# Column norms at the transitions of a fused two-block kernel, sums of squares in a PSUM bank, and a first merge in another order

## The reference, cut to what matters

```python
# first block
mix = merge(o_na, o_g, og, m_a, m_b, ...)      # w_branch_gla @ o_g and w_branch_na @ o_na, each gated, added, then @ w_out
x = x + g1 * mix
h2 = modulate(rmsnorm(x, norm2_g), sh2, sc2)
x = x + g2 * swiglu(h2, w_ffn_gate, w_ffn_up, w_ffn_down)
# second block, two layers l
h = rms_norm(x, ln_mix_pre[l]); proj = h @ w_in[l]
...
x = x + rms_norm(merged @ w_out[l], ln_mix_post[l])
h = rms_norm(x, ln_ffn_pre[l])
f = (silu(h @ ffn_w_gate[l]) * (h @ ffn_w_up[l])) @ ffn_w_down[l]
x = x + rms_norm(f, ln_ffn_post[l])
```

## Time and profile before

| | |
|---|---|
| median of 3 runs | 2956.88 us (2954.95 to 2958.97) |
| the profiled execution | 2956.38 us, span 2954.6 us |
| TensorE busy | 2825.1 us, 96% |
| VectorE, ScalarE, GpSimd busy | 1304.8, 1128.9, 1214.7 us |
| mean granted TensorE clock | 0.983 of 2.4 GHz |

### The profile page before, as it was taken

How to read it: one execution, slowest core, us unless ns; L and a number is a source line. 1 busy time by engine, 2 the same in 40 slices (tenths; PEclk the granted TensorE clock), 3 DMA queues, 4 the chain that set the end, 5 groups by cost and what they waited for, 6 DMA issues and landing times.

```text
span 2954.6 us, 34001 instructions
## 1 busy us (share of the span) xinstructions
PE 2825.1 (96%) x13512; PEld 2235.4 (76%) x13512; DVE 1304.8 (44%) x1679; ACT 1128.9 (38%) x1655; POOL 1214.7 (41%) x555
## 2 busy tenths in 40 slices
PE   7999999899999999999999999979999999899997
PEld 5787677688887776777777888857757868778886
DVE  4776414511113767835325202277777343431123
ACT  4334643332233555433334222245544233432221
POOL 2122233444444662443434444445624434444442
PEclk9999999999999999999999999999999999999999
DMA  6343222232223211122232222222102213222221
GB/s 251 115 160 118 72 83 103 89 113 100 93 100 123 75 62 42 69 90 73 91 114 79 100 93 96 98 100 73 65 29 79 95 69 110 84 96 98 98 94 64
DMA packets 88990, 277.44 MB, mean 94 GB/s; under 512 B 9920, under 2 KB 10240, under 8 KB 88832
## 3 DMA queue, kind: packets, MB, share of 16 engines
q1 hardware_dynamic: 88832, 275.26, 26.5%
HBM read 267.88 MB, written 7.34 MB: 93 GB/s over the span
## 4 chain that ended last, share of the span: by engine, by line
PE 84%; DVE 11%; ACT 3%; issue 1%; DMA 0%; SPq 0%; POOL 0%; DVEq 0%; ACTq 0%; POOLq 0%
PE bank L1490 25%; PE bank L1491 24%; PE bank L1492 24%; PE bank L1548 2%; PE bank L1733 2%; PE bank L1683 1%; PE bank L1695 1%; PE bank L1535 1%; PE bank L1724 1%; DVE pageF L2572 1%; DVE pageF L2576 1%; DVE pageR L2370 1%; DVE pageF L2502 1%; DVE pageF L2059 1%; DVE pageF L2070 1%
## 5 line engine op out<-in xcount | busy, mean ns | idle before, releaser
L2608 POOL TENSOR_TENSOR wlo<-wraw,whi 128x1024 fp32r<-128x1024 f32 x429 | 1043.6, 2434 | 1452.6 <-ACT whi L1762 1452.4
L1490 PE MATMUL bank<-pageR,whi 128*128 128x512 f32 x3552 | 1444.4, 407 | 53.7 <-ACT pageR L1947 22.1
L1492 PE MATMUL bank<-pageR,wlo 128*128 128x512 f32 x3552 | 1382.2, 389 | 0.0
L1491 PE MATMUL bank<-pageR,whi 128*128 128x512 f32 x3552 | 1381.9, 389 | 0.0
L1490 PEld LDWEIGHTS bank<-pageR,whi 128*128 128x128 f32 x3552 | 674.4, 190 | 234.6 <-issue 95.1
L1491 PEld LDWEIGHTS bank<-pageR,whi 128*128 128x128 f32 x3552 | 674.8, 190 | 153.4 <-issue 25.5
L1492 PEld LDWEIGHTS bank<-pageR,wlo 128*128 128x128 f32 x3552 | 673.3, 190 | 139.5
L1762 ACT ACTIVATE whi<-wraw 128x1024 fp32r<-128x1024 f32 x429 | 450.6, 1053 | 407.7 <-PE bank L1492 399.3
L1823 ACT ACTIVATE pageR<-pageF 128x512 fp32r<-128x512 f32 x136 | 85.9, 632 | 458.8 <-DVE pageF L2364 207.3
L2502 DVE SCALAR_TENSOR_TENSOR pageF<-pageF,prm 128x497 f32<-128x497 f32 (+9 forms) x180 | 198.1, 1100 | 2.7
L2617 POOL TENSOR_TENSOR pageR<-pageF,pageR 128x512 fp32r<-128x512 f32 x46 | 65.9, 1446 | 146.9 <-ACT pageR L1823 137.1
(11 more groups left out here) (205 smaller groups left out, 1983.8 us busy)
## 6 DMA issues: line engine op xcount, KB each, us to landing
wraw<-in_wst SPq DMA_DIRECT2D x429, 512.0 KB, 3.4
pageF<-in_wmod SPq DMA_DIRECT2D x96, 256.0 KB, 4.8
pageF<-in_xT SPq DMA_DIRECT2D x16, 256.0 KB, 4.3
pageF<-in_bias SPq DMA_DIRECT2D x16, 256.0 KB, 3.9
kept<-pageF SPq DMA_DIRECT2D x16, 256.0 KB, 5.1
pageF<-kept SPq DMA_DIRECT2D x16, 256.0 KB, 4.1
out_x<-pageF SPq DMA_DIRECT2D x8, 256.0 KB, 2.0
pageF<-in_cT SPq DMA_DIRECT2D x4, 256.0 KB, 7.4
```

Of the source, the lines that this page charges most:

```text
L1490: e.matmul(o, hi, xh, start=first, stop=False)
L1491: e.matmul(o, hi, xl, start=False, stop=False)
L1492: i = e.matmul(o, lo, xh, start=False, stop=last)
L2608: e.tensor_tensor(wlo[:, b % NH, :, :], wraw[:, b % NR, :, :], bc(whi[:, b % NH, :, :]), ALU.subtract).then_inc(*wlod.up(("wlo", b)))
```

## The change

It has six parts.

1. `branch_one` for the linear attention is the last part of the main chain of the weave, so the side chains' last steps are planned between its products; `main_gates1` hands back the pages of H.
2. The first four outputs of the first `w_out` go through `wide` input by input, in three banks of `sbk` and one of `mb`; their `x_add` and squares come after it.
3. `rstd_rows` takes the place of `rstd` in `norm_x2` and `post_norm`. `square_rows` multiplies each 128x128 block of the squares by one column of ones (four for the sum, four for the last square), which leaves a token's sum in one partition, 4 columns in all. `root` adds the two sets and takes the root on 4 columns. `spread` multiplies the root, broadcast over 128 columns, by the identity, which puts it into all partitions of the bank again; the users read the bank and not a page. `keep_warm` plans a product without a use: one between `square_rows` and `spread`, three after it.
4. The sum of an input's squares is kept in a bank of `sbk`, all seven additions are on VectorE, and GpSimd has none.
5. `wide` plans the input's norm (`late`) after the last product of input 6, ahead of the last four products.
6. Group 2 of the first block's ffn takes its banks from `sbk` too.

```diff
-    def wide(self, items, xs, ctx=None, late=None, feed=()):
+    def wide(self, items, xs, late=None, feed=(), homes=None):
...
+        outs = [(homes[i] if homes else self.mb).take(("o", *item)) for i, item in enumerate(items)]
         for k in range(8):
             next(feed, None)
             for (name, m), o in zip(items, outs):
                 s = self.w_next((name, m, k))
+                self.step("mm", s, ((o, xs[k]),), k == 0, k == 7)
+                if late is not None and k == 6 and o is outs[-1]:
+                    late()
                 yield
-        if late is not None:
-            late()
+    def keep_warm(self, bks, n):
+        self.warm += 1
+        bks.take(("warm", self.warm))
+        self.step("keep_warm", self.warm, n)
+        bks.give(("warm", self.warm), ("warm", self.warm))
+    def rstd_rows(self, n, bks):
+        p, t = self.p, self.tag
+        bks.take(("qm", t))
+        p.step("square_rows", t, self.n, self.tail)
+        for i in (0, self.tail):
+            p.pages.give(("q", t, i), ("qm", t))
+        p.pages.take(("r", t))
+        p.pages.take(("rt", t))
+        p.step("root", t, n)
+        p.keep_warm(bks, 1)
+        p.step("spread", t)
+        p.pages.give(("r", t), ("rs", t))
+        p.pages.give(("rt", t), ("rr", t))
+        p.keep_warm(bks, 3)
+        return ("qm", t)
...
+    weave(chain(main_gla(), main_og(), main_na(), free_context(), main_gates1(),
+                branch_one("o_gla", "w_branch_gla", "w_mb", None)),
+          [chain(side_gla(), side_na()), side_na_norm(), side_mod()], 1)
...
+    homes = [sbk, sbk, sbk, mb]
+    run(p.wide([("w_out", m) for m in range(4)], M, homes=homes))
     for m in range(8):
-        run(proj("w_out", m, M))
+        if m >= 4:
+            run(proj("w_out", m, M))
...
-        r = sq.rstd(1024, "ones", sbk)
+        r = sq.rstd_rows(1024, sbk)
...
-                    bks = sbk if rs is not None and j == 2 else mb
+                    bks = sbk if j == 2 else mb
...
             if m > 0:
+                acc = ("qb", self.gain)
+                if m == 1:
+                    sbk.take(acc)
                 step("in_sum", self.gain, m)
...
-            r = sf.rstd(1024, "ones", mb)
+            r = sf.rstd_rows(1024, sbk)
...
+            def square_rows(t, n, tail):
...
+                for c, i in ((0, 0), (4, tail)):
+                    w.wait_ge(*when("q", t, i))
+                    for j in range(4):
+                        x = e.matmul(o[:, c + j:c + j + 1], F(("q", t, i))[:, 128 * j:128 * j + 128], ones[:, 0:1],
+                                     start=True, stop=True)
+            def spread(t):
+                o, r = bank(("qm", t)), F(("r", t))
+                w.wait_ge(*when("rr", t))
+                for j in range(4):
+                    x = e.matmul(o[:, 128 * j:128 * j + 128], r[:, j:j + 1].broadcast_to([128, 128]), ident, start=True,
+                                 stop=True)
+            def keep_warm(i, n):
+                clear(("warm", i))
+                for _ in range(n):
+                    x = e.matmul(bank(("warm", i)), ident, cst[:, 0:4, :], start=True, stop=True)
...
+            def root(t, n):                                   # ScalarE
+                w.wait_ge(*when("qs", t))
+                e.activation(r, x, ACT.Ln, scale=1.0 / n, bias=col("eps")).then_inc(*fun.up())
+                e.activation(r, r, ACT.Exp, scale=-0.5).then_inc(*fun.up(("re", t)))
...
+            def root(t, n):                                   # VectorE, all on 4 columns
+                e.tensor_copy(s, o[:, 0:4]).then_inc(*vec.up())
+                e.tensor_tensor(x, s, o[:, 4:8], ALU.add).then_inc(*vec.up(("qs", t)))
+                e.scalar_tensor_tensor(s, r, -0.5 / n, r, ALU.mult, ALU.mult).then_inc(*vec.up())
+                e.scalar_tensor_tensor(s, x, n * EPS, s, ALU.add, ALU.mult).then_inc(*vec.up())
+                e.scalar_tensor_tensor(r, s, 1.5, r, ALU.add, ALU.mult).then_inc(*vec.up(("rr", t)))
...
             def in_sum(gain, m):
-                if m not in (2, 5, 7):
-                    return
...
+                first, acc = F(("q", t, 0)), bank(("qb", gain))
+                e.tensor_tensor(first if m == 7 else acc, first if m == 1 else acc, F(("q", t, m)), ALU.add).then_inc(
+                    *vec.up(("qa", t, m)))
...
-                e.scalar_tensor_tensor(y, y, col(gain, m), F(r), ALU.mult, ALU.mult).then_inc(*vec.up())
+                e.scalar_tensor_tensor(y, y, col(gain, m), bank(r), ALU.mult, ALU.mult).then_inc(*vec.up())
...
-            mine = {f.__name__: f for f in (w_split, halves, in_sum, tap)}
+            mine = {f.__name__: f for f in (w_split, halves, tap)}
```

More of the change, by code:

```diff
@@ L163, in __init__ @@
         self.pages, self.mb, self.sbk = Homes(NPAGE), Homes(4), Homes(4)
-        self.loaded = self.split = 0
+        self.loaded = self.split = self.warm = 0
         self.made = set()
@@ L206, in wide @@
             next(feed, None)
-        outs = []
-        for name, m in items:
-            o = [self.mb.take(("o", name, m))]
-            if ctx is not None:
-                o.append(self.mb.take(("oc", name, m)))
-            outs.append(o)
+        outs = [(homes[i] if homes else self.mb).take(("o", *item)) for i, item in enumerate(items)]
         for k in range(8):
@@ L846, in norm_x2 @@
                 yield
-        pages.give(r, ("h2s", 7))
+        sbk.give(r, ("h2s", 7))
     def main_ffn(sfx, xs, on_out, feed, rs=None):
@@ L957, in main_mla @@
                 step("load_table", name, l)
[L958 removed]
+            yield from p.wide([("w_kv" + L, 0), ("w_cq" + L, 0), ("w_cq" + L, 1), ("w_kpe" + L, 0)], X,
                               rs.rms, feed)
@@ L1244, in post_norm @@
                 if m == 7:
-                    pages.give(r, (*ver, 7))
+                    sbk.give(r, (*ver, 7))
                 yield
@@ new lines, in vector @@
+                mod_sum, mod_last, gated, gate_add, x_add, h2_hi, h2_lo, ffn_act, ffn_act_scaled, in_lo, in_sum,
+                pos_float, trig, decay_logs, scaled, tanh_scaled, rope_kpe, mla_q, mla_k, rope_scaled, rope_ret,
+                kv_normed, cq_normed, glu, tap, conv_bias, conv_mean, conv_silu, ret_centre, ret_gate, ret_decay,
+                ret_scores, ret_normed, post_norm, ffn_sum)}
+            for kind, *what in p.steps:
+                if kind in mine:
+                    mine[kind](*what)
@@ new lines, in gpsimd, with clear, w_split, halves @@
+        def gpsimd(e):
+            w = Hand(e)
+            def clear(name):
+                for k in over(name):
+                    w.wait_ge(*when(*k))
+            def w_split(b):
+                if b >= NH:
+                    w.wait_ge(*when("wdone", b - NH))
+                w.wait_ge(*when("wraw", b))
+                w.wait_ge(*when("whi", b))
+                e.tensor_tensor(wlo[:, b % NH, :, :], wraw[:, b % NR, :, :], bc(whi[:, b % NH, :, :]),
+                                ALU.subtract).then_inc(*wlod.up(("wlo", b)))
+            def halves(x, src, made, lane):
+                if lane != "pool":
+                    return
+                clear((*x, "lo"))
+                w.wait_ge(*when(*made))
+                w.wait_ge(*when(*x, "hi"))
+                e.tensor_tensor(R((*x, "lo")), F(src), bc(R((*x, "hi"))), ALU.subtract).then_inc(
+                    *low.up((*x, "lo")))
+            def tap(l, m, n, j):
+                if n == 0 or m < 3:
+                    return
+                s = j - 15
+                lo, hi = max(0, -s), min(T, T - s)
+                clear(("tap", l, n))
+                w.wait_ge(*when("glu", ("ca", l, m)))
+                e.activation(F(("tap", l, n))[:, 0:hi - lo], F(("ca", l, m))[:, lo + s:hi + s], ACT.Copy,
+                             scale=col(f"w_dw{l}", 31 * m + j)).then_inc(*fun.up(("tap", l, n)))
+            def conv_silu(l, m):
+                loaded[0] = None
+                x = F(("conv", l, m))
+                w.wait_ge(*when("cn", l, m))
+                e.activation(x, x, ACT.Silu, bias=col(f"cln_b{l}", m)).then_inc(*fun.up(("cs", l, m)))
+            def ret_gate(l, h, i):
+                loaded[0] = None
+                clear(("rg", l, h, i))
+                w.wait_ge(*when("rgp", l, h, i))
+                e.activation(F(("rg", l, h, i)), F(("rgp", l, h, i)), ACT.Tanh, scale=0.5).then_inc(
+                    *fun.up(("rg", l, h, i)))
+            def ret_decay(l, h):
+                lf, lb = (lg[:, 8 * l + 4 * x + h:8 * l + 4 * x + h + 1] for x in range(2))
+                w.wait_ge(*when("tabA"))
+                w.wait_ge(*when("lg"))
+                for i in range(2):
+                    clear(("tE", l, h, i))
+                    e.activation(F(("tE", l, h, i))[:, 0:448], rA2[:, 448 * i:448 * i + 448], ACT.Exp,
+                                 scale=lb).then_inc(*fun.up(("tE", l, h, i)))
+                if l or h:
```

(10 more changed lines are left out.)

551 lines of the change are left out of this document (534 added, 17 removed).

## The result

The changed kernel takes 2920.74 us (median of 4 runs, 2919.69 to 2921.46); beside it the kernel before took 2957.36 us (2954.95 to 2958.97). The ratio is 0.9878, with a 95% interval from 0.9862 to 0.9893: some 36 us faster. The forecast was 2923.5 us, with a range from 2914 to 2938.

What follows compares the result with a forecast made beforehand. TensorE, busy 96% of the span, was taken to set the time, so gains lie where it waits or runs at the lower clock. Terms 1.7 + 6.8 + 5.75 + 0.5 + 5.0 + 3.8 + 4.5 + 4.8 = 32.9; 2956.4 - 32.9 = 2923.5 us, range 2914 to 2938.

Steps and rivals of the forecast that it cites:

- 1, the branch: Linear-attention branch joins the main chain, its products covering the neighborhood attention's last steps: gain 1.7 us, bounds 1.0 and 2.0.
- 2, `w_out`: First `w_out`, four outputs input by input: both waits for late merged inputs go; gain 6.8 us, bounds 6.0 and 7.0.
- 3, column norms: Five norms: last square to first norm operation falls from 4.88 to 3.7 us; gain 1.15 each, 5.75 in all.
- 0.5 for the clock: At x1: half-clock starts cost 1.2 us; with warm-up products 0.5 us of gain was counted.
- in return the first products after the rest start at full clock: Behind the norms: warm-up products cost nothing at 2.4 GHz and spare the following products a half-clock start.
- the clock falls all the same: Rival, chance 0.14: tiny and spreading products at the norms may not hold the clock; about 11 us less gain, 2934.5.
- the warm-up products end after the first lower part: Sign that the prediction is wrong: behind a norm, warm-up products outlast the first input's lower part; no size given.
- 4, sums in a bank: Feeds: additions on VectorE are paid by the stretch beside GpSimd's sums that goes; 25.6 us becomes 23.8, 1.8 less.
- The higher fixed cost of a bank source: Counterargument on sums in a bank: 120 cycles against 58, 3.6 us less gain over three feeds; not used in the sum.
- 5, the norm before the last four products: Earlier input norm ends the wait for the first latent's square: 5.0 us at first layer, 3.8 at layer 1, 4.5 elsewhere.
- from 33.6 to 30.1: Other two feeds: us from first norm operation to the products' end, before and after; of 3.5, 2.25 taken each.
- 6, group 2: First block's ffn: the 3.0 us wait for a bank and 1.8 us of clock behind it go; gain 4.8 us.

Runs made afterwards that it cites:

- e11: The changed kernel with the first merge as before: linear-attention branch after the weave, eight outputs of `w_out` one after the other; 2928.18 us.
- e1: The changed kernel without its 20 warm-up products; column sums, root and spreading product stay; 2924.24 us.
- e8: The changed kernel with more cover at the five norms: 256-column warm-up products in the gaps and around the spreading product; 2919.09 us.
- e3: The changed kernel with the sums of an input's squares in a page again, four of seven on GpSimd; 2927.34 us.
- e4: The changed kernel with the input's norm planned after the last product of the eighth input again, in all four uses; 2930.29 us.
- e7: The changed kernel with scaled block and new x made in a bank in the three feeds behind a post-norm, ScalarE copying x to its page; 2910.99 us.
- e6: The changed kernel with squares summed in a page again, partly on GpSimd, and the full-width norm without spreading and warm-up products; 2938.38 us.
- e12: The changed kernel with group 2 of the first block's ffn in the first pool's banks again; 2923.77 us.
- e2: The changed kernel with the full-width norm of before in the five places, no spreading and no warm-up products; 2926.54 us.

## Why the prediction was right

The time was 2.8 us below the forecast and the mechanisms named were mostly the ones at work, but several terms were wrong by 2 to 3 us each and made up for one another. That the total came so close is in part luck.

**1, the branch** (1.7): 1.6. **2, `w_out`** (6.8): 7.0. Both by the working as it stood; e11 undoes these two alone and loses them.

**3, column norms** (5.75, and 0.5 for the clock): three terms of the sum failed. A place is worth 0.88 us and not 1.15, since 3.7 us was 4.01: the rows of the sum (tiny products) were still running when the last square ended, so it is 1.1 us and not 0.95 to their end, and the spreading product took 1.16. At x1 the norm gained nothing: its spreading product ran at 1.2 GHz, and the first user came at the same distance from the last `x_add` as before. And "in return the first products after the rest start at full clock" is true at C and E but worth nothing there (e1), as a feed is bound by VectorE. The rival "the clock falls all the same" came true in two of five places, x1 and D, at 0.9 (against e8) and 0.5 us and not 11 in all. In other traces of the same code it cost 2.8 at x1 and 0.9 each at D and at the end. One of the prediction's own signs of being wrong was met at these two places: the warm-up products end after the first lower part (549.91 against 549.64 at x1, 1907.24 against 1907.03 at D). It cost nothing there: TensorE's first product starts as soon as in e1 at x1 (8.79 us after the last of `w_out`), and at D 3.66 us after the first norm operation, as at C. In e3 and e4, where they took 4.8 us at x1, they held it by 1.6 us, the size that the prediction gave for the lower clock.

**4, sums in a bank** (1.8 us a feed): 1.2, 1.5 and 1.1. It took 23.1 us from the first norm operation (1530.46) to the end of the seventh lower part (1553.53), after a forecast of 23.8. The vector sums took 0.69 us, none of the 28 stretched (group mean of the form that reads and writes the bank 689 ns):

```profile
L3297 DVE SCALAR_TENSOR_TENSOR pageF<-pageF,prm,bank 128x512 f32<-128x512 f32 x32 | 23.7, 739 | 5.7 <-PE bank L1586 5.7
...
L3104 DVE TENSOR_TENSOR bank<-bank,pageF 128x512 f32<-128x512 f32 x20 | 13.8, 689 | 0.0
```

The rule of the Trainium skill (SBUF — State Buffer, Who interferes with whom) holds in these rows, and e7 agrees with it. The higher fixed cost of a bank source in the Trainium skill (VectorE: DVE Perf Modes, The TRN2 errata) is not to be seen: 689 ns against the 0.69 us of an unstretched add of two SBUF tensors.

**5, the norm before the last four products**: 4.6 at layer 0 (5.0) and 3.7 at layer 1. For the other two feeds the prediction took 2.25 us each "from 33.6 to 30.1". This step was wrong: it counted the time to the end of the first outputs, but the products behind them don't wait for those, and e4 shows the move to be worth nothing there. The feeds gained 4.0 and 3.8 all the same, 1.1 to 1.2 by the sums alone and the rest by sums and the new norm together (e6): with either of them TensorE's last wait in the feed is at most 1.7 us, with neither it is 2.1 and takes the clock with it. That a scaling which reads its factor from a bank no longer stretches was not in the prediction at all.

**6, group 2** (4.8): 1.6 by e12. This term failed by two thirds: the wait before had two causes, and the prediction took it all for the bank's. The other cause, the stretched step in front of the activation, went without a part aimed at it; e12 still gains 4.5 us in this stage without the banks. x1 and the ffn together gave 6.1, forecast 6.5, and that is luck: nothing by the norm, 1.6 by the banks, and 4.5 us for which the sum had no term.

So the sum of 32.9 stands against 35.1 in the trace (0.1 less at the branch and 0.2 more at `w_out` aside): -1.5 at the column norms outside x1, -0.4 at x1 and the ffn, -0.4 at layer 0, +1.7 and +1.6 in feeds C and E, +2.3 at D, and -1.2 of clock in stretches that no part touches. It did not contain the stretch of lower parts as a thing that could be removed; e7 shows 10 us of it left.

## What to carry to other kernels

Where one engine makes inputs for another one by one, look at which of its operations read two tensors from SBUF while a third engine works: moving one operand of each into a bank paid more (some 10 us in e7) than making the step before the feed shorter (0.9 us a norm) or keeping the clock up (nothing in the feeds). Count a saving at the engine that waits, not at the moment an output is ready: an output that nobody waits for is worth nothing sooner. And undo parts in pairs, too: two causes that hide each other read as zero, or as little, when undone alone (e2, e3 and e6). Where the clock can fall by chance, compare a stage with several kernels that are alike there before giving its time to an edit.

## What the runs showed of the hardware

Additions and scalings of 512 columns by VectorE with one tensor from SBUF and one from a bank kept their 0.69 to 0.75 us in every trace (at most 0.76 us), where two SBUF inputs took up to 2.9 us beside GpSimd. But one SBUF input alone is no protection: the step that holds a value between two constants (a TENSOR_SCALAR from page to page, L2401) took 2.50 us beside a split in the kernel before and 0.43 in e12. The Trainium skill (SBUF — State Buffer, Who interferes with whom) names this exception, for operations in a two-port mode.

The clock fell at x1 behind a gap of 0.80 us between tiny products (128x1) although records fill most of that time, and stayed at 1.00 through a feed with rests of 1.24, 1.08 and 1.70 us. The same rest of 2.7 us cost 2.0 us more in one trace than in the other (window 255 to 265). With the same code at D the spreading product ran at 2.4 GHz in e4 (1.16 us) and at 1.2 GHz in e3 (2.07 us). Runs of the kernel before lay between 2951.5 and 2959.9 us over all comparisons; that the clock's chance is the reason was not shown, but it is what the stages that don't repeat have in common.
